# Filler matmuls on constants, a later bias transpose and a reordered tile norm in a two-model kernel on one core

## The chip, the cores and the metric

One core of one Trainium2 chip runs the whole program in one launch. The metric is the device time in microseconds, the median of the runs. The core has five engines with queues of their own: TensorE (PE; its weight loads are listed as PEld), VectorE (DVE), ScalarE (ACT), GpSimd (POOL) and SyncE (SP, which here only issues DMAs). They meet at semaphores. TensorE's clock has two levels, 1.2 and 2.4 GHz; the profile tells the granted one as a share of 2.4 (1.00 or 0.50, or between for a stretch that has both).

## The reference

Two models one after the other, all in float32. The first block has two layers over 256 latent tokens and, in layer 0, 256 context tokens, each 1024 wide. The second block has two layers over the 256 latent tokens.

```python
# first block, layer l
mod = silu(c) @ w_ada[l] + b_ada[l]                   # 6 x 1024 shifts, scales, gates; the same for c_ctx
h = modulate(rms_norm(x, norm1_g[l]), sh1, sc1)
y = mixer(h)       # w_in; Fourier mix, global and window attention; gated branches; w_out
x = x + g1 * y
h = modulate(rms_norm(x, norm2_g[l]), sh2, sc2)
aff = softmax(h @ w_router[l])                        # 16 experts
top_aff, top_idx = top_k(aff.T, 32)                   # each expert picks 32 of 256 tokens
out = (silu(xg @ w_gate_e) * (xg @ w_up_e)) @ w_down_e * top_aff
x = x + g2 * scatter_add(out)
# second block, layer l
h = rms_norm(x, attn_norm_g[l])
x = x + (three kinds of attention over h @ w_in, gated) @ w_out[l]
x = x + cross_attention(rms_norm(x, xattn_norm_g[l]), mem) @ w_xo[l]
```

Between the two blocks stands the first block's final norm with `final_g`, after the second a last one.

## The kernel before

Tokens lie in tiles of 128 partitions: tiles 0 and 1 are the latent set (set 0), 2 and 3 the context (set 1, layer 0 alone). All weights pass through a ring of four SBUF slabs of 2 MB. A list (`slab_plan`) sets their order; SP issues the load of slab i as soon as slab i - 4 was released, which TensorE does with `last_release` after its last matmul on it. The instruction order of every engine is written out by hand; a wait holds up all that stands behind it on its engine.

**Start (lines 2670 to 2681, 671 and 842).** ScalarE's queue loads the condition vectors and gains into `vec1`, then biases and norm gains into `vec0` and `PAIRED`. `turn_vectors` on TensorE turns `vec1` and then, after a wait for the second group of loads (`ld_vec0`), `PAIRED` twice and `vec0`. VectorE copies the first result, forms CT (the silu of the conditions), and then makes `vec0t` from the second with one copy and six small ones; all of that stands ahead of `mixer(0)`. There TensorE runs the products of the modulation: `ada_product(n)` multiplies CT with a slab of `w_ada`, 32 matmuls with 32 columns of weights each, listed as 64 instructions; a copy (`ada_row`), a transpose (`ada_turn`) and an addition of the bias (`ada_column`) follow. Products 0 and 2 come first, then the transposes of the normed tiles (`first_turn`), then `first_part`, the first projection.

**Ahead of the experts (lines 1051 to 1103).** In both layers TensorE turns tile 0, runs an ada product (18 or 22), `logits(0)`, `turn_tile(1)`, `ada_turn` and `logits(1)`: 8 matmuls of 16 columns against the router's weights, listed as 16 instructions. VectorE forms the softmax, and with a chain of small operations on 16 partitions (`eight` four times, `threshold`, `slots`) the list of tokens for each expert; `turn_slots` turns it, `first_selection` makes a 0/1 matrix of it, and `gather` multiplies with that. In layer 0 the context set goes first, so that `turn_slots(1)` and `gather(0, 1, h)` stand between the latent set's logits and its own `turn_slots(0)` and `gather(0, 0, h)`; ada products 19, 20 and 21 lie between. In layer 1 there is one set, product 23 and `scaled_rows`, which spreads the gate vector over the partitions. Then come the experts: per expert six slabs, four of gate and up weights (line 1146), two of down weights (line 1181).

**The second block (lines 1226 to 1484, 1847 to 1857, 2575 to 2590).** Each layer begins with the norm `n3` of both tiles: ScalarE squares and sums a tile and takes the root (`normed` in its program), VectorE scales it (`normed` in its own), TensorE turns it in eight transposes, and the two engines scale half of the turned blocks each into `HT2` (`gained`). The first group of the projection, G30, needs tile 0 alone. In layer 0 both tiles come from the first block's final norm. In layer 1 tile 1's X gets its last addition only from the last matmuls of the layer before (line 1366), tile 0's is complete before; both ScalarE and VectorE norm tile 1 before they scale tile 0's turned halves:

```python
            else:                                     # ScalarE, layer 1
                normed("n3@1", 0, XN2, [read("X00", 0), read("X10", 0)])
                normed("n3@1", 1, XN2, [at("xo_rd@0", 2)])
                gained("n3@1", 0, HT2, 24)
```

`unit` is the identity and `bars` holds attention masks, both in bf16 and constant from line 2087 on (but for two parts of `bars` that are not read by the change).

Of the kernel before, what the change touches and what calls it, by code (L numbers as in the profile page):

```python
# [23 lines left out]
P = 128  # L24
D = 1024
KC = D // P
SEQ = 256
DEPTH = 2
# [5 lines left out]
COL = 512  # L34
# [129 lines left out]
def build(nc, a, out, ctx):  # L164
# [11 lines left out]
    def at(name, value):  # L176

        return sem(name), value + signal(name)[1]
# [24 lines left out]
    vec0t = sb("vec0t", P)  # L203
# [467 lines left out]
    def _(pe):  # L671
        def turn_vectors():
            pe.wait_ge(*at("ld_vec1", 16 * VEC1_LOADS))
            pe.transpose(ps[1][:, 0:64], vec1[0:64, :], ident[0:64, 0:64]).then_inc(sem("vec_turned"), 1)
            pe.wait_ge(*at("ld_vec0", 16 * VEC0_LOADS))
# [38 lines left out]
        def last_release(pe):  # L714
            pe.drain().then_inc(slab_used, 1)  # L715

# [122 lines left out]
        def mixer(l):  # L839
            tokens = 4 * P if l == 0 else 2 * P  # L840
            if l == 0:
                ada_product(0)
                ada_turn(0)
                ada_product(2)
                for t in range(4):
                    for k in range(6):
                        first_turn(k, t)
# [100 lines left out]
        def experts(l):  # L948
# [130 lines left out]
            ada_turn(first, 2)  # L1079
            logits(1)  # L1080
            if l == 0:
# [9 lines left out]
            else:  # L1091
# [3 lines left out]
                scaled_rows()  # L1095
                turn_slots(0)
            gather(0, 0, 0)
# [123 lines left out]
        def block2(l):  # L1221
# [160 lines left out]

            pe.wait_ge(*at(f"n3@{l}_xn", 1))
            turn_tile(f"n3@{l}", 0, XN2)
            tile_ready(f"n3@{l}", 0)
# [100 lines left out]
        turn_vectors()  # L1486
# [10 lines left out]
    def _(act):  # L1497
# [275 lines left out]
        def block2(l):  # L1773
# [76 lines left out]
            else:  # L1850
                normed("n3@1", 0, XN2, [read("X00", 0), read("X10", 0)])
                normed("n3@1", 1, XN2, [at("xo_rd@0", 2)])
                gained("n3@1", 0, HT2, 24)
# [92 lines left out]
    def _(dve):  # L1946
# [82 lines left out]

        def rotate(v, cos, sin, h, w, temps):  # L2030
# [12 lines left out]
        def mixer(l):  # L2043
            tiles = range(4) if l == 0 else range(2)
            tokens = 4 * P if l == 0 else 2 * P
            if l == 0:
                n1_normed(0, 0)
                ada_row(0)
                n1_normed(0, 1)
# [372 lines left out]
        def block2(l):  # L2422
# [162 lines left out]
            normed(f"n3@{l}", 1, XN2)  # L2585
            for t in range(2):
                gained(f"n3@{l}", t, HT2, 16 + 8 * l)
# [85 lines left out]
        dve.wait_ge(*at("vec_turned", 2))  # L2673
        link(dve.tensor_copy(vec0t[:, :], ps[0][:, 0:P]))
        pairs_in = ps[0][:, P:P + 48].rearrange("p (i l n q) -> p l n q i", i=2, l=DEPTH, n=3)
        for l in range(DEPTH):
            for n, c in enumerate((24, 32, 56)):
                ins = dve.tensor_copy(vec0t[:, 64 * l + c:64 * l + c + 8].rearrange("p (q i) -> p q i", i=2),
                                      pairs_in[:, l, n])
        link(ins)  # L2680
# [67 lines left out]
```

## Time and profile before

| | us |
|---|---|
| three runs | 2294.29, 2292.11, 2294.47 |
| median | 2294.29 |
| the profiled execution | 2297.57 |
| its span, first to last instruction | 2295.7 |
| TensorE busy in the span | 1981.8 (86%) |
| VectorE, ScalarE busy | 623.4 (27%), 435.2 (19%) |
| mean granted clock | 0.961 |
| from HBM | 573 MB, 250 GB/s over the span |

A row of the timeline gives the start, the duration, the engine, the line, the operation, what it writes and reads, and in brackets how long the engine had been idle and what ended that. Neighbouring instructions of one line are merged (x16). A row of the stretches gives each engine's busy time, the granted clock (PEclk) and what the DMA moved. The duration of a pipelined matmul is longer than its distance to the next.

### The profile page before, as it was taken

What the parts mean: (1) busy time and instruction counts of PE and PEld (TensorE: products, weight loads), DVE (VectorE), ACT (ScalarE), POOL (GpSimd) and SP (SyncE); (2) the same over time, 40 slices, a digit from 0 to 9 for tenths busy, and PEclk for the clock granted to TensorE, in tenths of its full rate; (3) what the DMA queues carried; (4) which work ended last, traced back from release to release, by engine and by line L of the source; (5) the groups of instructions that cost most, each with busy time, mean ns of one, the idle gap of its engine ahead of it and who ended that gap; (6) DMA issues with size and microseconds to landing.
All of it is one profiled execution on the core that took longest, in us unless ns stands there. A gap on an engine that the chain in (4) does not pass through costs nothing.

```text
span 2295.7 us, 31442 instructions
## 1 busy us (share of the span) xinstructions
PE 1981.8 (86%) x13540; PEld 1088.4 (47%) x13540; DVE 623.4 (27%) x1483; ACT 435.2 (19%) x1095; POOL 26.9 (1%) x52
## 2 busy tenths in 40 slices
PE   6999999998988898889999975676776699989997
PEld 4445554455434444335768641233432247564765
DVE  2012640234112222213351321201110235323533
ACT  2112621013111111002261111100000212222222
POOL 3000000000000000000000000000000000000000
PEclk9999999999999999999999988889989899999999
DMA  8554245227899999994415589999999833233320
GB/s 288 183 175 157 73 147 183 74 73 277 344 423 422 422 422 421 416 418 149 147 46 187 217 348 423 424 415 416 417 414 418 333 110 110 103 118 110 110 83 19
DMA packets 133831, 576.01 MB, mean 251 GB/s; under 512 B 7448, under 2 KB 16128, under 8 KB 92736
## 3 DMA queue, kind: packets, MB, share of 16 engines
q1 hardware_dynamic: 129312, 556.82, 61.5%
q0 software_dynamic: 3872, 17.00, 2.2%
q8 instruction: 109, 1.79, 0.3%
q10 hardware_dynamic: 512, 0.19, 0.0%
q14 instruction: 26, 0.21, 0.0%
HBM read 572.93 MB, written 1.05 MB: 250 GB/s over the span
## 4 chain that ended last, share of the span: by engine, by line
PE 51%; DMA 20%; issue 10%; PEld 8%; DVE 5%; PEldq 3%; ACT 2%; SPq 0%; ACTq 0%; DVEq 0%
DMA ring<-w_up_e 15%; PE ps L781 8%; PE ps L1237 5%; PE ps L1146 5%; PE ps L964 4%; DMA ring<-w_down_e 3%; PE ps L1245 3%; PEld ps L1181 3%; PEldq L715 3%; PE ps L797 2%; PE ps L1379 2%; PE ps L770 2%; PEld ps L1015 1%; PE ps L1216 1%; PE ps L1322 1%
## 5 line engine op out<-in xcount | busy, mean ns | idle before, releaser
L1146 PE MATMUL ps<-ring,reg_bc 128*32 128x512 f32 x2960 | 381.8, 652 | 132.9 <-DMA ring<-w_up_e 124.8
L1146 PEld LDWEIGHTS ps<-ring,reg_bc 128*32 128x32 f32 x2960 | 91.6, 115 | 398.7 <-DMA ring<-w_up_e 208.1
L781 PE MATMUL ps<-reg_a,ring 128*128 128x512 f32 (+1 forms) x768 | 253.9, 488 | 6.1 <-issue 4.4
L781 PEld LDWEIGHTS ps<-reg_a,ring 128*128 128x128 f32 x768 | 143.5, 190 | 105.2 <-issue 92.2
L2323 DVE TENSOR_TENSOR xall<-xall,ps 128x512 f32<-128x512 f32 x48 | 32.8, 687 | 447.5 <-PE ps L1112 447.5
L1237 PE MATMUL ps<-ring,reg_a 128*128 128x512 f32 (+2 forms) x448 | 146.0, 482 | 7.4 <-issue 5.9
L1744 ACT ACTIVATE reg_bc<-ps 128x512 f32<-128x512 f32 x48 | 28.7, 597 | 571.2 <-PE ps L1146 571.2
L2366 DVE TENSOR_TENSOR reg_a<-ps,reg_e 32x256 f32<-32x256 f32 x192 | 80.7, 420 | 197.4 <-PE ps L1181 195.0
L1181 PE MATMUL ps<-ring,reg_bc 128*32 128x256 f32 x2048 | 117.4, 380 | 15.7 <-issue 13.3
L770 PE MATMUL ps<-ring,reg_a 128*128 128x512 f32 (+1 forms) x288 | 112.8, 546 | 1.9 <-issue 1.5
L1237 PEld LDWEIGHTS ps<-ring,reg_a 128*128 128x128 f32 x448 | 75.2, 193 | 72.2 <-issue 69.1
L1245 PE MATMUL ps<-reg_a,ring 128*128 128x256 f32 x384 | 90.7, 396 | 6.1 <-ACT reg_d L1782 5.0
L1181 PEld LDWEIGHTS ps<-ring,reg_bc 128*32 128x32 f32 x2048 | 69.7, 110 | 54.4 <-issue 19.4
L1181 PE MATMUL ps<-ring,reg_e 128*32 128x256 f32 x1024 | 63.4, 389 | 33.2 <-issue 17.6
L964 PE MATMUL ps<-ring,reg_bc 128*128 128x512 f32 x192 | 86.0, 604 | 0.6 <-issue 0.5
L797 PE MATMUL ps<-reg_d,ring 128*128 128x512 f32 (+1 forms) x256 | 84.2, 488 | 1.7 <-issue 0.8
L1245 PEld LDWEIGHTS ps<-reg_a,ring 128*128 128x128 f32 x384 | 75.2, 199 | 17.6 <-issue 7.0
L770 PEld LDWEIGHTS ps<-ring,reg_a 128*128 128x128 f32 x288 | 54.2, 190 | 56.2 <-issue 54.6
L797 PEld LDWEIGHTS ps<-reg_d,ring 128*128 128x128 f32 x256 | 48.1, 190 | 35.6 <-issue 30.4
L1552 ACT ACTIVATE reg_e<-ps 128x512 f32<-128x512 f32 (+1 forms) x48 | 23.6, 491 | 208.5 <-PE ps L781 208.4
L1181 PEld LDWEIGHTS ps<-ring,reg_e 128*32 128x32 f32 x1024 | 33.3, 111 | 56.4 <-issue 24.4
L566 DVE TENSOR_REDUCE st<-ps 128x2 f32<-128x1024 f32 (+1 forms) x36 | 37.5, 1046 | 82.7 <-PE ps L498 79.8
(354 smaller groups left out, 2145.7 us busy)
## 6 DMA issues: line engine op xcount, KB each, us to landing
ring<-w_down_e SPq DMA_DIRECT2D x64, 2048.0 KB, 15.2
ring<-w_gate_e SPq DMA_DIRECT2D x123, 1024.0 KB, 10.6
ring<-w_up_e SPq DMA_DIRECT2D x123, 1024.0 KB, 13.9
ring<-w_in SPq DMA_DIRECT2D x34, 2048.0 KB, 8.3
ring<-w_ada SPq DMA_DIRECT2D x24, 2048.0 KB, 8.1
ring<-w_out SPq DMA_DIRECT2D x8, 2048.0 KB, 8.1
ring<-w_xkv SPq DMA_DIRECT2D x8, 1024.0 KB, 14.1
ring<-w_br_global SPq DMA_DIRECT2D x4, 1024.0 KB, 6.2
```

Source lines behind the costliest of these rows:

```text
L566: ins = dve.tensor_reduce(neg, banks_of(2 * (i % 2), u["nk"]), X_AXIS, ALU.max, negate=True)
L715: pe.drain().then_inc(slab_used, 1)
L770: mm = pe.matmul(ps[t][:, c0:COL], HT[:, k, t * P:t * P + P], w[:, k, c0:COL], start=(k == 0), stop=(k == KC - 1))
L781: mm = pe.matmul(ps[j][:, 0:n], w[:, k, j * P:(j + 1) * P], HT[:, k, 0:n], start=(k == 0), stop=(k == KC - 1))
L797: mm = pe.matmul(ps[n % 4][:, 0:tokens], w[:, k, j * P:(j + 1) * P], OT[:, k, 0:tokens], start=(k == k0), stop=(k == k1 - 1))
L964: mm = pe.matmul(ps[b][:, :], MT[:, k, t * P:t * P + P], w[:, k, :], start=(k == 0), stop=(k == KC - 1))
L1146: mm = pe.matmul(ps[s][32 * j:32 * j + 32, :], XGT[l][:, e // 4, s, 2 * q + k, e % 4 * CAP:(e % 4 + 1) * CAP], w[j // 2][:, k, (j % 2) * C ...
L1181: mm = pe.matmul(ps[4 + s][32 * j:32 * j + 32, 0:SEQ], HE[l][:, s, k, q * CAP:(q + 1) * CAP], w[:, k, j * SEQ:(j + 1) * SEQ], start=(q == ...
L1237: fill(name, lambda b: [pe.matmul(ps[b][:, 0:c1 - c0], src[:, k, t * P:t * P + P], w[:, k, c0:c1], start=(k == 0), stop=(k == KC - 1)) for ...
L1245: fill(name, lambda b: [pe.matmul(ps[b][:, 0:SEQ], w[:, k, c * P:(c + 1) * P], src[:, k, :], start=(k == 0), stop=(k == KC - 1)) for k in ...
L1379: yield pe.matmul(ps[b][:, :], OT2[:, k, t * P:t * P + P], w[:, k, :], start=(q == 0), stop=(q == KC - 1))
L2366: ins = dve.tensor_tensor(OE[l][r:r + CAP, e // 4 % 2, s, j * SEQ:(j + 1) * SEQ], ps[4 + s][CAP * j:CAP * (j + 1), 0:SEQ], GB[CAP * j:CAP ...
```

## The change

It adds `keep_warm(b, n)` to TensorE's program: n matmuls with `unit` as stationary and 256 columns of `bars` as moving operand, into the second half of PSUM bank b, read by nobody. It is called at seven places: between `ada_turn` and `logits(1)` (24 in layer 0, 10 in layer 1), after `logits(1)` (10), in layer 1 after `scaled_rows` (8) and after `turn_slots(0)` (6), ahead of the second block's first wait in layer 0 (45), and after tile 0's transposes in both of its layers (14). `turn_vectors` is split: the condition vector is turned first as before, the biases only after `ada_product(0)`; their copies on VectorE move behind `ada_row(0)`, and TensorE waits for them after `ada_product(2)`. At the second block's second layer, ScalarE and VectorE scale tile 0's halves ahead of tile 1's norm.

```diff
-        def turn_vectors():
+        def turn_condition():
             pe.wait_ge(*at("ld_vec1", 16 * VEC1_LOADS))
             pe.transpose(ps[1][:, 0:64], vec1[0:64, :], ident[0:64, 0:64]).then_inc(sem("vec_turned"), 1)
+
+        def turn_biases():
             pe.wait_ge(*at("ld_vec0", 16 * VEC0_LOADS))
...
+        def keep_warm(b, n):
+
+            for _ in range(n):
+                pe.matmul(ps[b][:, SEQ:COL], unit[:, :], bars[:, 0:SEQ], start=True, stop=True)
...
                 ada_product(0)
+                turn_biases()
                 ada_turn(0)
                 ada_product(2)
+                pe.wait_ge(*at("vec0t", 1))
                 for t in range(4):
...
             ada_turn(first, 2)
+            keep_warm((4, 6)[l], (24, 10)[l])
             logits(1)
+            keep_warm((4, 6)[l], 10)
...
                 scaled_rows()
+                keep_warm(6, 8)
                 turn_slots(0)
+                keep_warm(6, 6)
             gather(0, 0, 0)
...
+            if l == 0:
+                keep_warm(7, 45)
             pe.wait_ge(*at(f"n3@{l}_xn", 1))
             turn_tile(f"n3@{l}", 0, XN2)
+            keep_warm(7, 14)
             tile_ready(f"n3@{l}", 0)
...
-        turn_vectors()
+        turn_condition()
...
                 normed("n3@1", 0, XN2, [read("X00", 0), read("X10", 0)])
+                gained("n3@1", 0, HT2, 24)
                 normed("n3@1", 1, XN2, [at("xo_rd@0", 2)])
-                gained("n3@1", 0, HT2, 24)
...
                 n1_normed(0, 0)
                 ada_row(0)
+                bias_columns()
                 n1_normed(0, 1)
...
-            normed(f"n3@{l}", 1, XN2)
-            for t in range(2):
-                gained(f"n3@{l}", t, HT2, 16 + 8 * l)
+                normed("n3@0", 1, XN2)
+                gained("n3@0", 0, HT2, 16)
+            else:
+                gained("n3@1", 0, HT2, 24)
+                normed("n3@1", 1, XN2)
+            gained(f"n3@{l}", 1, HT2, 16 + 8 * l)
```

`bias_columns` holds the seven copies that stood ahead of VectorE's layers, with the wait for the transposes before them and a signal (`vec0t`) behind.

## Rows read from the trace of the kernel before

**Rows 1.** The page: the chain that ended last, by engine, and GB/s in 40 slices.
```profile
PE 51%; DMA 20%; issue 10%; PEld 8%; DVE 5%; PEldq 3%; ACT 2%; SPq 0%; ACTq 0%; DVEq 0%
...
GB/s 288 183 175 157 73 147 183 74 73 277 344 423 422 422 422 421 416 418 149 147 46 187 217 348 423 424 415 416 417 414 418 333 110 110 103 118 110 110 83 19
```

**Rows 2.** Timeline of the start: SP's first issues, TensorE's transposes, products, first projection.
```profile
0.74 1.06 SPq L602 DMA_DIRECT2D ring<-w_ada  x2
...
16.20 0.43 PE L677 MATMUL ps<-ident,reg_e 24*128 24x24 f32 x2 [5.42 <-DMA reg_e<-norm_g]
...
16.97 3.64 PE L695 MATMUL ps<-ring,ct 128*32 128x128 f32 x64
...
21.43 2.45 PE L695 MATMUL ps<-ring,ct 128*32 128x128 f32 x64
...
24.03 2.83 PE L744 MATMUL ps<-ident,reg_d 128*128 128x128 f32 x24
...
28.58 7.10 PE L755 MATMUL ps<-ring,reg_a 128*128 128x512 f32 x16 [1.61 <-ACT reg_a L1513]
```

**Rows 3.** Ring loads, issue to landing: those under way in 0 to 1, 1 to 1.5 us.
```profile
DMA to landing us min/median/max: 13.0/13.0/13.0
...
DMA to landing us min/median/max: 13.0/16.0/18.9
```

**Rows 4.** Timeline of TensorE ahead of layer 0's experts.
```profile
529.86 1.93 PE L982 MATMUL ps<-wr,reg_a 128*128 128x16 f32 x16 [0.32 <-issue]
...
536.50 3.56 PE L982 MATMUL ps<-wr,reg_a 128*128 128x16 f32 x16 [3.53 <-issue]
...
549.90 2.04 PE L695 MATMUL ps<-ring,ct 128*32 128x128 f32 x64 [0.31 <-ACT modt L1535]
...
552.13 0.29 PE L997 MATMUL ps<-ident,reg_e 16*128 16x16 f32 x2 [0.18 <-DVE reg_e L2233]
...
553.24 4.04 PE L1015 MATMUL ps<-tmp,reg_d 128*128 128x128 f32 x32 [0.55 <-DVE tmp L2240]
```

**Rows 5.** Stretches: busy time of PE, PEld, DVE, ACT, POOL; PEclk, DMA share, GB/s.
```profile
1308.00:1312.00 4.00, 2.71 (x18) 2.26 (x17) 2.10 (x5) 2.12 (x8) 0.00 (x0) 0.67 1.01 424
...
1332.00:1336.00 4.00, 4.00 (x31) 2.56 (x30) 0.00 (x0) 2.77 (x8) 0.00 (x0) 0.85 0.00 0
...
1338.00:1800.00 462.00, 311.38 (x2408) 138.88 (x2408) 57.62 (x146) 37.92 (x84) 0.00 (x0) 0.88 1.01 418
...
2061.00:2064.00 3.00, 3.00 (x6) 1.21 (x5) 0.00 (x0) 0.00 (x0) 0.00 (x0) 0.55 0.23 85
```

**Rows 6.** Timeline of TensorE ahead of layer 1's experts.
```profile
1311.96 3.57 PE L982 MATMUL ps<-wr,reg_a 128*128 128x16 f32 x16 [1.29 <-ACT reg_a L1669]
...
1327.68 0.27 PE L997 MATMUL ps<-ident,reg_e 16*128 16x16 f32 x2 [1.11 <-DVE reg_e L2233]
...
1328.77 5.57 PE L1015 MATMUL ps<-tmp,reg_d 128*128 128x128 f32 x32 [0.81 <-DVE tmp L2240]
```

**Rows 7.** Timeline at the second block's first layer: last X addition, tile 0's transposes, G30.
```profile
1815.62 0.69 DVE L2323 TENSOR_TENSOR xall<-xall,ps 128x512 f32<-128x512 f32 x1 [0.17 <-PE ps L1112]
...
1821.98 1.94 PE L1256 MATMUL ps<-ident,reg_d 128*128 128x128 f32 x8 [6.41 <-DVE reg_d L2446]
...
1825.19 8.58 PE L1237 MATMUL ps<-ring,reg_a 128*128 128x512 f32 x16 [1.27 <-ACT reg_a L1787]
```

**Rows 8.** Timeline at the second block's second layer: transposes, VectorE's half, G30.
```profile
2054.75 1.09 PE L1256 MATMUL ps<-ident,reg_d 128*128 128x128 f32 x8
...
2058.39 1.12 DVE L2440 TENSOR_SCALAR reg_a<-ps,vec1t 128x128 f32<-128x128 f32 x4
2059.62 8.80 PE L1237 MATMUL ps<-ring,reg_a 128*128 128x512 f32 x16 [3.77 <-issue]
```

**Rows 9.** The bf16 mask matmuls: durations (min/median/max ns) by line, four in the timeline.
```profile
L1279 PE MATMUL ps<-bars,unit x80: 219/219/230, 1864.8 to 2200.1; 128*128 128x128 bf16 x80
...
1864.81 0.40 PE L1279 MATMUL ps<-bars,unit 128*128 128x128 bf16 x4
```

## What the change should do to the time: a prediction

> **What bounds the kernel now.** First the page: its chain of waits gives TensorE half of the span and the DMA a fifth [rows 1], and the row of GB/s shows two plateaus near 420, the two expert stages, with weaker slices before and after. From 1338 to 1800 us the DMA moves 418 GB/s without a pause [rows 5]: there a faster TensorE buys nothing. What comes before such a plateau still counts, if the stream is waiting for TensorE: from 1332 to 1336 it moved 0 GB/s [rows 5], since no ring slab had been released. The same holds for layer 0, where slices 9 and 10 (516 to 631 us) stand at 277 and 344 GB/s [rows 1]. So I read the timeline at the five places that the diff touches, and beside it the granted clock in the table by stretches. At each, TensorE waits, its clock falls from 2.4 to 1.2 GHz, and the work behind the wait pays for it: 16 matmuls of the logits take 1.93 us at full clock and 3.56 at half [rows 4], 16 of the projection 7.10 [rows 2] against 8.58 and 8.80 [rows 7, 8].
>
> **What a filler costs.** None is in the trace. Its nearest relative is the bf16 mask matmul of 128 columns on the same stationary `unit`: one alone lasts 0.22 us and four in a row 0.40, so each further one costs (0.40 - 0.22) / 3 = 0.06 us [rows 9]. A filler has 256 columns: 0.11 us at full clock, 0.23 at half. 10 cost 1.1, 14 cost 1.6, 24 cost 2.7, 45 cost 5.1 us. They read constants and write halves of banks that nobody reads then, so nothing but TensorE's own queue is behind them.
>
> **Start.** Before, three bias transposes stand ahead of the first ada product and wait 5.4 us for the last small load, until 16.20; the product starts at 16.97 [rows 2]. Its slab was there at 0.74 + 13.0 = 13.7 us [rows 2, 3]. Now it runs 13.8 to 17.4, the biases follow without a wait, and the second product starts when its slab lands, 18.9 us after an issue at about 1.2 us [rows 3]: 20.1 instead of 21.43. VectorE's seven short bias copies move behind `ada_row(0)`; TensorE's new wait `vec0t` has all the first transposes queued behind it, but stands behind the second product, which can't start before 20.1 and so covers the copies; without that cover they would hold the transposes up by their own length. In exchange TensorE, which had nearly unbroken work from 16.97, now has 2.7 us between the products with only four small transposes in it. The second product took 2.45 before [rows 2]; a product costs 3.64 at half clock and 2.04 at full [rows 2, 4]. At 3.64 it ends at 23.8, as before (23.9); at 2.04, 1.7 us earlier; and if the clock is still low behind it, the 24 transposes cost up to 2.8 us more [rows 2]. Ends: +1.7 and -2.8. I take -0.2, by the row of the cold product, since a pause comes in where the clock had been rising. On SP's queue the first released slab's load is issued earlier, but behind three loads that are still under way (18.9 us to landing [rows 3]), so it lands no earlier.
>
> **Layer 0 before the experts.** The 24 fillers (2.7 us) stand in an idle stretch of 3.53 us ahead of the second logits [rows 4]. They hold the clock: 3.56 becomes 1.93, +1.6. The next ten (1.1 us) delay `turn_slots(1)`, for which VectorE's first selection waits, with token set 0's top-k queued behind it: -0.3. The third ada product gets faster, but VectorE's chain to the second `slots` is what TensorE waits for; so what is late next is that chain, and TensorE, about 1.5 us ahead of it, now idles there after its product of 549.90 [rows 4]. Before, it had no gap there (552.13 with 0.18 us of waiting). No filler covers this new gap, and behind it stand gathers of 4.04 us [rows 4]; in layer 1 the same work took 5.57 with the clock partly low [rows 6]. Ends: +1.6 and, with gathers wholly at half clock, about -2.5. I take +1.3 - 1.5 = -0.2.
>
> **Layer 1 before the experts.** The clock is already falling before the first ten fillers (0.67 from 1308 to 1312 [rows 5]), so they cost up to 2.3 us in a gap of 1.29 [rows 6]: the logits start 1.0 late and then take 1.93 instead of 3.57: +0.6. The second ten lie beside the softmax; the 8 beside VectorE's chain, where TensorE idles 1.11 us; the 6 (0.7 us) in the 0.81 us before the gather [rows 6]. The gathers should take 4.04 [rows 4] instead of 5.57 [rows 6]: +1.5. I take +2.0; ends 0 (clock lost twice) and 3.1 (never lost). It passes to the end, since the stream starts with the first slab released.
>
> **First seam of the second block.** The last X addition ends at 1816.3; TensorE transposes again at 1821.98 [rows 7]. 45 fillers end at 1821.4, so they fit; if that cover went, their excess would be paid in full. The 8 transposes fall from 1.94 to about 1.09 [rows 7, 8], of which I count 0.4, since VectorE's norm of tile 1 still stands ahead of its half of the copies. The 14 more (1.6 us) lie beside the copies. G30's 8.58 becomes 7.10: +1.5. Sum +1.9; ends +0.4 and +2.4.
>
> **Second seam.** Here the order changes too. Tile 0 is transposed from 2054.75 to 2055.84; VectorE scales its half only at 2058.39, for 1.12 us, behind tile 1's norm, and G30 starts at 2059.62 [rows 8]. Now both halves follow the transposes: 2055.9 + 1.12 = 2057.0; the 14 fillers end at 2057.3. G30 starts 2.3 earlier and takes 7.10 instead of 8.80 (clock 0.55 in 2061 to 2064 [rows 5]): +1.7. Tile 1's norm starts about 1 us later on both engines, since each now scales tile 0 first, but TensorE asks for it only after G30, 7 us on. Together +4.0; ends +2.0 (the order alone, with 0.3 lost) and +4.2.
>
> **Sum.** -0.2 - 0.2 + 2.0 + 1.9 + 4.0 = 7.5 us. The profiled execution took 2297.57, so it would be 2290.1; the median of the runs before is 2294.29, 3.3 less, and I carry that difference over: **2286.8 us**. Its own range, with one or two places falling well or badly: 2284 to 2289.7. This kernel's measurement can tell about 0.2% (4.6 us) from no change.
>
> **Rivals.**
> Everything holds: the upper ends, but in layer 0 the 1.3 without the gap's cost: 1.7 + 1.3 + 3.1 + 2.4 + 4.2 = 12.7 gives 2281.6. Against it: the new gap in layer 0. Chance 0.11.
> Transposes don't count as work for the clock. The trace shows 8 transposes in 1.09 us where 8 others took 1.94 [rows 7, 8], so they follow the clock, not whether they hold it. If they do nothing for it, the second seam is bridged by 14 fillers alone and the start has 24 transposes with nothing to lift the clock: 1.7 and, as the middle of what cold transposes cost, 1.3 less: total 4.5, 2289.8. Chance 0.10. The Trainium skill, page "TensorE: Matmul & The Clock Gate", section "Part 4: PE-mode transpose", states that the full clock does not engage for transposes, which don't count as busy in the same way; by that rule this case is the one, while the trace at least contradicts that they run slow.
> The start and layer 0 fall badly (-2.8, -2.5) and layer 1 gives 0: with 1.9 and 4.0 at the seams 0.6 us, 2293.7. For it: in both places work was moved or shortened and an idle stretch of 2 to 3 us left behind it that no filler covers. Chance 0.11.
> The fillers don't hold the clock and only the new order pays: 2.3 - 0.3 = 2.0, 2292.3. Against it: unbroken small matmuls did raise the clock at the start, where one product took 3.64 and the next 2.45 [rows 2]. Chance 0.07.
> The other side, slower: the fillers run at 1.2 GHz, 0.23 us each. Then the 45 take 10.3 us in 5.6, 4.7 late, and the 14 behind them (3.2) 1.9 more than the copies beside them; in layer 0 24 take 5.5 in 3.5 and ten 2.3 against 1.2 that are hidden, 3.1; in layer 1 1.0 + 0.9 + 0.6 = 2.5; start 0.2; less 0.7 at the second seam: 11.7 slower, 2306.0. It decides at the first seam: above 5.6 / 45 = 0.125 us for one filler the change begins to lose. Against it: the bf16 row at full clock [rows 9], and TensorE works until 0.7 us before the 45. Chance 0.05.
>
> **Chances.** Forecast 0.56, the others as given. Range 2281.5 to 2292.5: it leaves out the bad case and the slower one, 0.16. Faster than 2289.7: 0.56 (less 0.01), 0.11 and half of the transpose case: 0.72. Slower 0.05, within 0.23.
>
> **What would show it.** Right: 45 fillers in about 5 us ending before 1821; G30 7.1 us at both seams, starting near 2057 less what was gained before; logits 1.93; layer 1's first slab released 2 us earlier against its start. Wrong: fillers over 0.125 us each; gathers at 553 above 5 us (then layer 0 has cost something, as I suspect) or at 4.04 (then I was too low); the 24 first transposes above 3 us.

## The result, and the profile after

The changed kernel took **2283.57 us** (median, 2280.98 to 2284.23) against 2294.38 for the kernel before on the same chip: ratio 0.995, 95% interval 0.9933 to 0.9967, so 10.8 us or 0.5% faster. A second comparison (the run `changed_again` below) gave 2281.87 against 2293.82, ratio 0.9955 (0.9942 to 0.9969). The prediction said 2286.8 with a range of 2281.5 to 2292.5, and faster with a chance of 0.72.

The profiled execution after took 2280.98 us (span 2279.1), the one before 2297.57. These two differ by 16.6 us, more than the medians; where the rest lies is a question of its own, taken up below. First the places that the diff touches. (`keep_warm` is called by six statements, not seven as said above; with both layers they run nine times.) All rows are of the timeline of TensorE: start and duration in us, line, operation, number of instructions, and in brackets the idle time ahead and what ended it.

The start, after:

```profile
13.50 3.64 PE L697 MATMUL ps<-ring,ct 128*32 128x128 f32 x64 [2.92 <-DMA ring<-w_ada]
...
20.12 3.64 PE L697 MATMUL ps<-ring,ct 128*32 128x128 f32 x64 [0.94 <-DMA ring<-w_ada]
24.06 3.68 PE L751 MATMUL ps<-ident,reg_d 128*128 128x128 f32 x24 [0.29 <-DVE reg_d L1992]
...
29.45 4.10 PE L762 MATMUL ps<-ring,reg_a 128*128 128x512 f32 x9 [1.60 <-ACT reg_a L1529]
```

The first product now starts at 13.50, as soon as its slab has landed, and the second at 20.12, 1.3 us earlier than before [rows 2]. But both take 3.64 us, and the transposes behind them 3.68. That this is the half clock can't be read from the profile's column of the granted clock, which gives 1.00 for all of the start. Two other things show it. The same product took 3.64 us in the kernel before at 1317.50, where that column gives 0.50:

```profile
1317.50 3.64 PE L695 MATMUL ps<-ring,ct 128*32 128x128 f32 x64
```

```profile
1317.60:1321.00 3.40, 3.40 (x64) 2.86 (x64) 3.22 (x10) 0.12 (x1) 0.00 (x0) 0.50 0.95 390
```

And the trace's list of clock changes begins with a rise to full: at 22.5 us before, inside the second product, and at 25.9 after, inside the transposes. The projection starts at 29.45.

Layer 0 ahead of the experts, after:

```profile
529.82 2.78 PE L722 MATMUL ps<-bars,unit 128*128 128x256 bf16 x24
533.49 1.93 PE L991 MATMUL ps<-wr,reg_a 128*128 128x16 f32 x16 [0.89 <-issue]
...
547.39 0.29 PE L1006 MATMUL ps<-ident,reg_e 16*128 16x16 f32 x2 [1.54 <-DVE reg_e L2262]
548.50 5.37 PE L1024 MATMUL ps<-tmp,reg_d 128*128 128x128 f32 x32 [0.55 <-DVE tmp L2269]
```

The 24 fillers take 2.78 us, 0.11 each, and the logits behind them 1.93 instead of 3.56 [rows 4]. The slots (L1006) now wait 1.54 us, which they did not before, and the gathers behind that wait take 5.37 instead of 4.04 [rows 4].

Layer 1 ahead of the experts, after, and two lines of the table by stretches (columns: stretch, length, busy time of PE, PEld, DVE, ACT and POOL with their instructions, granted TensorE clock, DMA share, GB/s):

```profile
1303.96 2.18 PE L722 MATMUL ps<-bars,unit 128*128 128x256 bf16 x10
1305.98 1.86 PE L991 MATMUL ps<-wr,reg_a 128*128 128x16 f32 x16
...
1319.68 0.39 PE L1006 MATMUL ps<-ident,reg_e 16*128 16x16 f32 x2 [2.81 <-DVE reg_e L2262]
1320.01 1.46 PE L722 MATMUL ps<-bars,unit 128*128 128x256 bf16 x6
1321.26 4.67 PE L1024 MATMUL ps<-tmp,reg_d 128*128 128x128 f32 x32
```

```profile
1303.00:1307.00 4.00, 4.00 (x26) 3.40 (x25) 1.37 (x4) 2.12 (x8) 0.00 (x0) 0.64 1.02 422
1807.00:1813.00 6.00, 5.09 (x45) 4.32 (x45) 5.62 (x17) 4.87 (x13) 0.00 (x0) 1.00 1.05 387
```

The clock is already down when the first ten fillers start, as it was before them before (0.64 in 1303 to 1307, against 0.67 [rows 5]); they take 2.18 us, almost twice their price, but the logits take 1.86 instead of 3.57 and the gathers 4.67 instead of 5.57 [rows 6]. The wait ahead of the slots (L1006) is not gone: it is 2.81 us, behind the eight fillers, where it was 1.11 [rows 6].

The first seam of the second block, after:

```profile
1807.53 5.09 PE L722 MATMUL ps<-bars,unit 128*128 128x256 bf16 x45 [0.78 <-DVE xall L2352]
1813.06 1.09 PE L1269 MATMUL ps<-ident,reg_d 128*128 128x128 f32 x8 [0.45 <-DVE reg_d L2475]
1813.99 1.69 PE L722 MATMUL ps<-bars,unit 128*128 128x256 bf16 x14
1815.90 7.11 PE L1250 MATMUL ps<-ring,reg_a 128*128 128x512 f32 x16 [0.21 <-issue]
```

45 fillers in 5.09 us, 0.45 us before the norm is ready; transposes 1.09 instead of 1.94, G30 7.11 instead of 8.58 [rows 7].

The second seam, TensorE and then VectorE:

```profile
2042.53 1.09 PE L1269 MATMUL ps<-ident,reg_d 128*128 128x128 f32 x8
2043.45 1.69 PE L722 MATMUL ps<-bars,unit 128*128 128x256 bf16 x14
2044.98 7.03 PE L1250 MATMUL ps<-ring,reg_a 128*128 128x512 f32 x16
```

```profile
2043.65 1.13 DVE L2469 TENSOR_SCALAR reg_a<-ps,vec1t 128x128 f32<-128x128 f32 x4 [0.50 <-PE ps L1269]
...
2046.50 0.81 DVE L2475 TENSOR_SCALAR reg_d<-xall,st 128x1024 f32<-128x1024 f32 x1
```

VectorE scales tile 0's half (L2469) right behind the transposes, and tile 1's norm (L2475) follows; G30 starts 2.45 us after the start of the transposes instead of 4.87 and takes 7.03 instead of 8.80 [rows 8].

**What one pair of traces can't say.** Of the 16.6 us, the places of the diff give 7.3 by the lengths below (-0.9, 0.4, 1.7, 1.8, 4.2). The other 9.3 lie where nothing was edited. The clearest such place is H4 and H5, 32 matmuls of the second block's projection, run in each of its layers, behind the same wait of 2.48 us in both traces, before and after:

```profile
1968.75 10.20 PE L1245 MATMUL ps<-reg_a,ring 128*128 128x256 f32 x32 [2.48 <-ACT reg_d L1782]
```

```profile
1957.99 8.73 PE L1258 MATMUL ps<-reg_a,ring 128*128 128x256 f32 x32 [2.48 <-ACT reg_d L1798]
```

Behind one and the same wait the clock may fall for a while (8.73) or for longer (10.20); traces further down show it stay as well (7.14). So each place has to be read in several executions, and the experiments gave these.

### The profile page after: what moved, and what is told of

Its sections match the earlier page's. It is cut to its first block, busy times and chain, and to the rows that moved or that the text cites. A ratio compares the mean times of both kernels' runs of the same rounds, so it can differ in the third digit from the quotient of the medians.

```text
span 2279.1 us, 31723 instructions
## 1 busy us (share of the span) xinstructions
PE 1986.8 (87%) x13681; PEld 1093.5 (48%) x13681; DVE 623.2 (27%) x1483; ACT 435.3 (19%) x1095; POOL 26.9 (1%) x52
## 4 chain that ended last, share of the span: by engine, by line
PE 53%; DMA 19%; issue 10%; PEld 8%; DVE 5%; PEldq 2%; ACT 2%; SPq 0%; POOL 0%; DVEq 0%; POOLq 0%
DMA ring<-w_up_e 14%; PE ps L788 8%; PE ps L1159 6%; PE ps L1250 5%; PE ps L973 4%; PE ps L1258 3%; PEld ps L1194 3%; PE ps L804 2%; PE ps L1392 2%; PE ps L777 2%; PEldq L717 2%; DMA ring<-w_xkv 2%; DMA ring<-w_down_e 2%; PE ps L1226 1%; PE ps L1229 1%
## 5 line engine op out<-in xcount | busy, mean ns | idle before, releaser
L1194 PE MATMUL ps<-ring,reg_bc 128*32 128x256 f32 x2048 | 117.8, 380 | 16.2 <-issue 14.7
L1194 PE MATMUL ps<-ring,reg_e 128*32 128x256 f32 x1024 | 67.2, 406 | 31.4 <-issue 17.6
L1194 PEld LDWEIGHTS ps<-ring,reg_e 128*32 128x32 f32 x1024 | 34.5, 116 | 57.1 <-issue 29.2
L1705 ACT ACTIVATE reg_bc<-ps,modt,scl 128x128 f32<-128x128 f32 x96 | 36.2, 458 | 129.2 <-PE ps L1024 129.2
```

Source lines behind the costliest of these rows:

```text
L1194: mm = pe.matmul(ps[4 + s][32 * j:32 * j + 32, 0:SEQ], HE[l][:, s, k, q * CAP:(q + 1) * CAP], w[:, k, j * SEQ:(j + 1) * SEQ], start=(q == ...
L1705: ins = act.activation(XGT[l][:, g, s, k, :], ps[6 + h][:, kk * P:(kk + 1) * P], ACT.Identity, scale=SCL[:, l, 1, k, s:s + 1], bias=MODT[: ...
```

## The experiments

**A place's length over all executions.** The lengths used below are: *start*, the time at which the first projection starts; *layer 0*, from the first tile's logits of the place to the first expert matmul; *layer 1*, from the transposes ahead of its logits to the first expert matmul; *first and second seam*, from tile 0's transposes to tile 1's. Each is read from the profiled execution of each kernel. The numbers in brackets are means. The kernels below that add fillers in a place or warm the start are left out of that place's row. The one whose fillers are transposes is in the rows of the start and the first seam only.

```
                 without the edit                     with the edit
start            28.58 28.14 28.0 27.2 27.76  (27.9)  29.45 27.0 28.47 28.60 29.65 28.41 28.37  (28.6)
layer 0          29.67 30.04 29.68 30.75 29.92 (30.0) 29.28 27.98 27.98 30.01 29.03 29.49       (29.0)
layer 1          30.77 31.44 31.49 31.41      (31.3)  29.04 28.98 29.11 29.66 29.23 and 4 like them (29.2)
first seam       11.62 11.95 12.20 11.88      (11.9)  9.76 to 9.78, nine executions
second seam      13.50 14.75 14.81           (14.35)  order alone 9.30, fillers alone 11.80, both 9.32
```

**The kernel before, once more.** No edit; a second trace of it.

> The kernel before, unedited, for a second trace of it. The first two traces (before 2297.57, after 2280.98) differ by 16.6 us where the medians differ by 10.8 to 12. Theory 1 (the rest is which of the unchanged pauses the clock fell behind in those two executions): this execution lies nearer to the median of 2294, and H4 and H5 at 1969, which took 10.20 us, come out at 7.1 or 8.8; the stretches that the diff touches keep their lengths within 1.5 us (layer 1's place 30.8, first seam 11.6, second seam 13.5). Theory 2 (the stretches differ by the kernel's own order, not by execution): the same 10.20 at H4 and H5, and the same stretch lengths within 0.3 us everywhere.

Measured: median 2294.87 (2292.07 to 2299.56) against 2294.73 for its twin, ratio 0.9999 (0.999 to 1.0008); the profiled execution took 2299.56. So "nearer to the median" was a miss, this was another long one. The lengths of the places were not the same within 0.3 us, which rules the second theory out (layer 1's place is 31.44 instead of 30.77, the second seam 14.75 instead of 13.50): H4 and H5 took 8.70 instead of 10.20, G30 at the second seam 10.06 instead of 8.80 [rows 8].

```profile
1970.94 8.70 PE L1245 MATMUL ps<-reg_a,ring 128*128 128x256 f32 x32 [2.48 <-ACT reg_d L1782]
...
2060.29 10.06 PE L1237 MATMUL ps<-ring,reg_a 128*128 128x512 f32 x16 [3.77 <-issue]
```

**The changed kernel, once more.** No edit.

> The changed kernel itself, unedited, as the measure for the other two kernels on the same chip. Ratio to the kernel before as in the first comparison, 0.995, within its interval of 0.9933 to 0.9967. If it stands at 0.997 or above, a part of the first 10.8 us was luck of which pauses the clock fell behind.

Measured: the ratio 0.9955 given above, as expected. Its trace bears on the suspicion about layer 0's new wait:

```profile
548.04 0.30 PE L1006 MATMUL ps<-ident,reg_e 16*128 16x16 f32 x2 [1.53 <-DVE reg_e L2262]
...
549.15 4.04 PE L1024 MATMUL ps<-tmp,reg_d 128*128 128x128 f32 x32 [0.55 <-DVE tmp L2269]
```

The same wait of 1.53 us, and the gathers take 4.04. Of the five traces in which that wait is there (1.25 to 1.54 us) and nothing fills it, three have 4.04 and two 5.37 and 5.57. The wait costs about 1.5 us in some executions and nothing in others. In two more traces the clock had fallen earlier, from the second logits on (2.3 us instead of 1.93); there the wait is gone (0.17 us), since TensorE comes later, and the gathers take 4.04. Of these seven traces only two, this one and that of the doubled fillers further down, held the clock through the whole place. They have its shortest length, 27.98; in the other five the clock fell somewhere, at the transposes, the logits, the fillers or the gathers, and the place took 29.0 to 30.0.

In layer 1 the same trace has all of it at full clock up to the slots, and the fall behind them:

```profile
1318.01 0.39 PE L1006 MATMUL ps<-ident,reg_e 16*128 16x16 f32 x2 [2.81 <-DVE reg_e L2262]
1318.34 1.46 PE L722 MATMUL ps<-bars,unit 128*128 128x256 bf16 x6
1319.59 5.67 PE L1024 MATMUL ps<-tmp,reg_d 128*128 128x128 f32 x32
```

Of the ten traces with layer 1's fillers, six have the first ten at half clock (2.2 to 2.3 us) and four at full (1.25). The gathers took 4.04 in one of the ten, 4.7 to 6.0 in the others, and longest (5.7 to 6.0) in the four whose first ten fillers had run at full clock. So the place is 29.0 to 29.7 us long either way.

**The start alone.** `turn_condition`, `turn_biases` and `bias_columns` as in the change; no fillers, the old order at the seam:

```diff
-        turn_vectors()
+        turn_condition()
...
                 ada_product(0)
+                turn_biases()
                 ada_turn(0)
                 ada_product(2)
+                pe.wait_ge(*at("vec0t", 1))
```

> The kernel before with the start's edit alone (biases turned behind the first ada product), no fillers, old order at the second seam. My account: no gain, between 0.9 us slower (as the first projection in the profile of the changed kernel, 29.45 against 28.58 us) and 0.5 faster; the second ada product begins near 20.1 us and takes 3.6, the 24 first transposes take more than the 2.83 us of before. Rival (the earlier products pay): the first projection begins at 27.2 or earlier and the whole is 1.4 to 1.7 us faster.

Measured: 2293.68 (2291.92 to 2297.12) against 2296.27, ratio 0.9992 (0.9984 to 1.0001): no change that can be told; the interval runs from 0.2 us slower to 3.7 us faster. In this execution the clock rose at 18.1, the second product took 1.96 and the projection started at 27.0, the best of all; in six others with this edit that product took 2.89 to 3.64 and the projection started at 28.4 to 29.7. In all five traces without the edit the second product took 1.95 to 2.45.

**The order alone.** Only ScalarE's and VectorE's order at the second seam:

```diff
                 normed("n3@1", 0, XN2, [read("X00", 0), read("X10", 0)])
+                gained("n3@1", 0, HT2, 24)
                 normed("n3@1", 1, XN2, [at("xo_rd@0", 2)])
-                gained("n3@1", 0, HT2, 24)
```

> The kernel before with the second seam's new order alone, no fillers. G30 begins 1.5 us after the transposes instead of 3.8. My account: 2.3 us from the order; whether the clock holds over the shorter idle stretch decides on another 1.6: 2.3 to 4.0 us faster than before. Rival (the fillers carry that seam): the clock falls there in this kernel too, G30 takes 8.6 us or more, and the whole is 2.3 us faster at most.

Measured: 2290.08 (2286.67 to 2293.24), ratio 0.9972 (0.9963 to 0.9982), 6.2 us by the medians, more than the 2.3 to 4.0 expected. The seam takes 9.30 us, 5.0 less than the mean of 14.35, with no filler in the kernel:

```profile
2048.13 1.09 PE L1261 MATMUL ps<-ident,reg_d 128*128 128x128 f32 x8
2050.48 7.11 PE L1242 MATMUL ps<-ring,reg_a 128*128 128x512 f32 x16 [1.26 <-ACT reg_a L1792]
```

A wait of 1.26 us is left, and G30 behind it runs at full clock. That is one trace, but the medians of eight runs agree: the interval begins at 4.1 us, above the 2.5 that the order gives without the clock.

**The fillers alone.** All calls of `keep_warm`, without the start's edit and with the old order.

```diff
+            keep_warm((4, 6)[l], (24, 10)[l])
             logits(1)
+            keep_warm((4, 6)[l], 10)
...
+                keep_warm(7, 45)
...
             turn_tile(f"n3@{l}", 0, XN2)
+            keep_warm(7, 14)
```

> The kernel before with all fillers, without the start's edit and the new order. My account by places: layer 0 +0.4 (gathers at 548 to 553 us partly at half clock), layer 1 +1.7, first seam +1.9, second seam +1.6 by the clock alone: 5.6 us faster. Rival (the changed kernel's 10.8 us come from fillers acting beyond their places): 8 us or more.

Measured: 2287.24 (2286.65 to 2288.18), ratio 0.9962 (0.9949 to 0.9975), 9.0 us (5.7 to 11.7), where 5.6 was expected and 8 or more by the rival. By the means in the table the places of this kernel give 1.0 + 2.2 + 2.1 + 2.6 = 7.9 us, so most of the difference is that the 5.6 was added up from one pair of traces; fillers that act beyond their places aren't needed for it. The second seam takes 11.80:

```profile
2046.09 1.09 PE L1265 MATMUL ps<-ident,reg_d 128*128 128x128 f32 x8
2047.02 1.69 PE L720 MATMUL ps<-bars,unit 128*128 128x256 bf16 x14
2050.95 7.11 PE L1246 MATMUL ps<-ring,reg_a 128*128 128x512 f32 x16 [2.24 <-issue]
```

Here the fillers end and a wait of 2.24 us for VectorE is left, which is what the new order takes away (11.80 - 9.32 = 2.5 us); G30 is at full clock in either kernel. So at this seam each half is enough for the clock, in the one trace that each has, and once the order is new, the 14 fillers show no gain of their own (9.30 without them, 9.32 with them).

**The change without the start's edit.**

```diff
-        turn_condition()
+        turn_vectors()
```

(with the rest of the start as before.)

> The changed kernel without the start's edit. If the start costs, as its profile says (0.9 us at the first projection), this is 0.9 us faster than the changed kernel, 11 to 12 us faster than before. If the start pays, it is 1 to 2 us slower than the changed kernel, 9 to 10 us faster than before.

Measured: 2284.32 (2279.28 to 2287.46), ratio 0.9946 (0.9933 to 0.996). The whole change had 0.995 and 0.9955: with or without the start's edit, no difference can be told.

**The change without layer 0's 34 fillers.**

```diff
-            keep_warm((4, 6)[l], (24, 10)[l])
+            if l:
+                keep_warm(6, 10)
             logits(1)
-            keep_warm((4, 6)[l], 10)
+            if l:
+                keep_warm(6, 10)
```

> The changed kernel without the 24 and the 10 fillers of layer 0; all others stay. It measures the term that the prediction took as -0.2 us (ends +1.6 and -2.5). Theory 1 (the prediction's): the second logits 3.56 instead of 1.93, no wait ahead of the second slots, gathers 4.04: within 0.5 us of the changed kernel. Theory 2 (the fillers of layer 0 gain, since what is late next is hidden better than I thought): 1 to 1.6 us slower. Theory 3 (they cost): up to 2.5 us faster than the changed kernel. In the profile: from the first logits of the place to the first expert matmul 29.3 us in the changed kernel (22.64 and 6.64) and 29.7 before.

Measured: 2285.39 (2282.95 to 2287.95) against 2281.87 for the changed kernel in the same runs, 3.5 us slower; the two intervals of their ratios overlap (0.9952 to 0.9977, and 0.9942 to 0.9969), so the size is not sure, but the sign agrees with the place: 29.92 us here, 30.0 in the mean of the five without these fillers, 29.0 in the mean of the six with them. The two groups overlap (29.67 to 30.75, and 27.98 to 30.01).

```profile
534.43 3.57 PE L991 MATMUL ps<-wr,reg_a 128*128 128x16 f32 x16 [3.53 <-issue]
...
550.27 0.29 PE L1006 MATMUL ps<-ident,reg_e 16*128 16x16 f32 x2
...
551.36 4.04 PE L1024 MATMUL ps<-tmp,reg_d 128*128 128x128 f32 x32 [0.50 <-DVE tmp L2271]
```

The rows of before are back: logits 3.57 behind an idle stretch of 3.53, and no wait at the slots, as both theories have it. The size is nearer to the second, with about 1 us by the place.

**Do transposes hold the clock?** Every filler becomes a transpose of the identity, their numbers unchanged:

```diff
-                pe.matmul(ps[b][:, SEQ:COL], unit[:, :], bars[:, 0:SEQ], start=True, stop=True)
+                pe.transpose(ps[b][:, SEQ:SEQ + P], ident[:, :], ident[:, :])
```

> The changed kernel with every filler made a transpose of the identity (float32, 128 columns) instead of a bf16 matmul, the numbers of them unchanged. Eight real transposes took 1.09 us in the changed kernel, so 45 should take 5.0 to 5.5 us, as the fillers' 5.09. Theory 1 (transposes keep the clock up as well as matmuls do; for it, the run with the order alone, where nothing but transposes stood between O and G30 and G30 still took 7.1): logits 1.93 in both layers, G30 7.1 at both seams, 2284 us, within 0.1% of the changed kernel. Theory 2 (transposes do not count, as the Trainium skill, page "TensorE: Matmul & The Clock Gate", section "Part 4: PE-mode transpose", states): the second logits of layer 0 back to 3.56, layer 1's logits to 3.57 and its gathers to 5.6, the first G30 to 8.6: 1.6 + 3.1 + 1.5 = 6 us slower, 2289.8.

Measured: 2285.25 (2283.91 to 2287.76), ratio 0.9963 (0.9951 to 0.9976).

```profile
1811.64 5.13 PE L722 MATMUL ps<-ident 128*128 128x128 f32 x45 [0.78 <-DVE xall L2352]
...
1820.01 7.10 PE L1250 MATMUL ps<-ring,reg_a 128*128 128x512 f32 x16 [0.20 <-issue]
```

45 transposes last 5.13 us, and G30 behind them 7.10. The places: layer 0 29.5, layer 1 29.2, seams 9.76 and 9.32, each as with matmuls. The first theory holds: float32 transposes keep the clock as well as bf16 matmuls do. The ratio is 0.0008 to 0.0013 above the changed kernel's, inside the intervals.

**Twice the fillers at the first seam.**

```diff
-                keep_warm(7, 45)
+                keep_warm(7, 90)
```

> The changed kernel with 90 fillers instead of 45 at the first seam. In the changed kernel 45 take 5.09 us from 1807.5 and the norm's first tile is ready at 1813.06. Theory 1 (a filler past its cover is paid in full, and the clock is full at either count): the 90 end at 1817.7, the transposes start 4.6 us later, G30 still takes 7.1: 2288.2. Theory 2 (what ends last at the seam is VectorE's or the DMA's chain, so an excess is partly hidden): under 2 us slower, 2284 to 2285.5. Theory 3 (fillers at half clock): 0.23 us each, the 90 take 20 us, 15 us slower.

Measured: 2288.83 (2285.26 to 2294.98), ratio 0.9975 (0.9964 to 0.9986), 0.20 to 0.25% above the changed kernel's ratios, which is 4.6 to 5.7 us; the intervals still touch.

```profile
1808.01 10.00 PE L722 MATMUL ps<-bars,unit 128*128 128x256 bf16 x90 [0.78 <-DVE xall L2352]
1817.85 1.04 PE L1269 MATMUL ps<-ident,reg_d 128*128 128x128 f32 x8
...
1820.25 7.03 PE L1250 MATMUL ps<-ring,reg_a 128*128 128x512 f32 x16
```

10.00 us for 90, the same 0.11 each. From the first expert matmul of layer 1 to the transposes it takes 491.4 us instead of 487.0 to 487.7 (488.7 in one of nine), and the seam behind 9.27 instead of 9.77: 3.7 us net, paid almost in full, as the first theory has it. The cover of 5.6 us is real and has 0.45 left.

**Three more waits filled.**

```diff
                 ada_product(20, 2)
+                keep_warm(6, 12)
                 turn_slots(0)
...
+            keep_warm(4, 20)
             columns("H4", "in2", 7, 2, HT2)
```

> The changed kernel with fillers in three more waits that the clock falls behind: 12 ahead of layer 0's second slots (they wait 1.54 us, and the gathers behind took 5.37 instead of 4.04), and in both layers 20 ahead of H4 in the second block (wait 2.48 us; H4 and H5 behind it took 8.73 and 8.59, where 32 such matmuls take 7.2 at full clock). Theory 1 (the fall follows from the pause right ahead, and filling it takes the fall away): gathers 4.04, H4 and H5 7.2, 1.3 + 1.5 + 1.4 = 4.2 us, 2279.4. Theory 2 (the falls are only moved on to the next pause): the same total as the changed kernel within 1 us. Theory 3 (the fillers run over their pause): 0 to 1 us slower.

Measured: 2284.04 (2282.85 to 2285.84), ratio 0.9956 (0.9945 to 0.9968): no better than the changed kernel. The two kinds of wait part:

```profile
537.80 2.26 PE L722 MATMUL ps<-bars,unit 128*128 128x256 bf16 x10
...
549.86 1.48 PE L722 MATMUL ps<-bars,unit 128*128 128x256 bf16 x12
...
552.38 4.04 PE L1024 MATMUL ps<-tmp,reg_d 128*128 128x128 f32 x32 [0.56 <-DVE tmp L2271]
```

```profile
1960.64 2.35 PE L722 MATMUL ps<-bars,unit 128*128 128x256 bf16 x20
1963.28 7.14 PE L1259 MATMUL ps<-reg_a,ring 128*128 128x256 f32 x32 [0.29 <-ACT reg_d L1800]
```

In layer 0 the gathers take 4.04, but the clock has fallen earlier, at the ten fillers behind the logits (2.26 us instead of 1.25), and the place is 29.3 us long, as without the twelve. That is what the second theory forecast, but it doesn't show it: this earlier fall stands ahead of the twelve, and traces without them have it too, so what they do to the clock stays open. Ahead of H4 the first theory holds. Without fillers, 22 executions of this stretch (eleven traces, two layers) gave 7.14 three times, 8.5 to 8.8 seventeen times and 10.20 twice, in the mean 8.65; with them, 7.14 in six of six. That is 1.5 us in each layer by the place. The median does not show these 3 us.

**The same, with the start warmed.** Float32 matmuls of the identity on itself ahead of the first product (12), and 3 and 4 around the transpose of its row:

```diff
+                warm_up(12)
                 ada_product(0)
                 turn_biases()
+                warm_up(3)
                 ada_turn(0)
+                warm_up(4)
                 ada_product(2)
```

> The kernel with the three filled pauses, and in addition float32 matmuls of the identity on itself at the start: 12 ahead of the first ada product, 3 before and 4 after the transpose of its row. Theory 1 (the clock rises before the first product): the products 2.04 us instead of 3.64, the second from 20.1 to 22.2, the first transposes limited by VectorE's last norm at 23.8, the first projection at 27.3 instead of 29.45: 2.2 us, 2277.2. Theory 2 (the gain at the start is taken back, since the projection's slabs or the vector engines' chain set what follows): projection starts earlier, but the first logits near 505 do not; 2279.4. Theory 3 (not enough work to lift the clock): products 3.6 each, no gain.

Measured: 2280.29 (2278.34 to 2284.02), ratio 0.9943 (0.993 to 0.9956), 3.75 us below the kernel without the warm start in the same runs, with intervals that overlap. The clock rose at 14.7 us. The products took 1.96 us each, the projection started at 27.09 and the first logits at 503.7; in the seven traces with the start's edit alone these logits start at 504.6 to 506.6. The 12 ran 4.85 us and held the first product up until 15.40, which cost nothing, since the second waits for its slab until 20.3.

**The warm start with 7, 1 and 3 matmuls, H4's fillers, nothing added in layer 0.**

```diff
-                warm_up(12)
+                warm_up(7)
...
-                keep_warm(6, 12)
                 turn_slots(0)
```

> The changed kernel with 20 fillers ahead of H4 in both layers, and float32 matmuls of the identity at the start (7 ahead of the first product, 1 and 3 around the transpose of its row; 0.40 us each where the clock was half, so 7 take 2.8 of the 2.9 us that TensorE waits for the slab). Nothing is added in layer 0 ahead of the slots. Theory 1 (both gains add, and the start's 2.3 us pass on to the end): H4 and H5 7.2 instead of 8.7 twice, 3.0, projection at 27.1 instead of 29.45, 2.3: 5.3 us below the changed kernel in the same runs. Theory 2 (the start's gain is taken back before the first logits): 3.0 us below it. Theory 3 (the falls of the clock move elsewhere): within 1 us of it.

Measured: 2282.47 (2278.13 to 2286.48), ratio 0.9952 (0.9938 to 0.9965), against 2281.87 for the changed kernel in the same runs.

```profile
10.62 3.35 PE L678 MATMUL ps<-ident 128*128 128x128 f32 x14
13.90 2.89 PE L701 MATMUL ps<-ring,ct 128*32 128x128 f32 x64
...
20.28 1.95 PE L701 MATMUL ps<-ring,ct 128*32 128x128 f32 x64 [0.58 <-DMA ring<-w_ada]
22.53 2.81 PE L755 MATMUL ps<-ident,reg_d 128*128 128x128 f32 x24 [0.29 <-DVE reg_d L2000]
...
27.06 6.26 PE L766 MATMUL ps<-ring,reg_a 128*128 128x512 f32 x14 [1.60 <-DMA ring<-w_in]
```

Its profiled execution, 2278.13 us, is the shortest seen, with projection at 27.06, logits at 503.6 and H4 at 7.14 twice, just what was expected place by place. The median of its five runs gives none of it: by the medians the third theory. Five runs of each, spread over 4 to 8 us, can't tell 5 us from nothing here, and `gaps_start` points the other way. Whether the two additions pay stays open, and so does how much of the start's gain reaches the first logits: these two traces have them at 503.6 and 503.7, but one without the start's edit and without any warming has them at 503.8, though its projection starts at 27.76.

## Why the prediction was right

**The price of a filler**: right. 0.11 us at full clock, in tens, 24s, 45 and 90; 0.22 at half. (The working as shown, 0.06 us for 128 columns, would give 0.12 for 256; the 0.11 is what was measured.)

**Start**, -0.2 with ends +1.7 and -2.8: the size was a little too kind, -0.7 by the mean of the projection's starts (27.9 to 28.6), with the spread that the ends gave (27.0 to 29.65). The step was right: the second product starts when its slab lands, and loses in the clock what it gains in time. That the clock is the cause is shown by the executions in which it rose early and stayed, at 18.1 in the start alone and at 14.7 and 15.9 with the warm start: there the same order reaches the projection at 27.0 and 27.1. In three more traces with this edit it rose at 16.4 to 17.6, but fell again at 19.8 to 21.0, about the pause between the products, and the second product took 2.9 to 3.5. What the step costs the whole kernel stays open: the start alone, with an interval of -0.2 to +3.7 us, doesn't show the loss of 0.7.

**Layer 0**, -0.2: the term that was most mis-sized; it is +1.0. The logits went from 3.56 to 1.93 and the new wait of 1.5 us appeared, both as worked out. The step that was off is the 1.5 taken for slow gathers: they come in two of seven traces. In three others the clock falls elsewhere in the place, and only two are free of a fall.

**Layer 1**, +2.0: 31.3 to 29.2, 2.1. The number is right, the way to it only in part, and that is luck. The sum had +1.5 for gathers at 4.04, and they took 4.04 in one of ten traces. The wait of 1.11 us ahead of the slots, which the eight fillers were to cover, was a row of one execution: in the other three traces without fillers it is 3.0, and with them 2.8 are left in nine of ten, the fall of the clock behind it. Without fillers the gathers took 5.57, 6.68, 6.59 and 6.74, so there was more to gain than the sum knew; and the logits gave more than the 0.6 where the first ten fillers ran at full clock, in four of ten. These errors cancel.

**First seam**, +1.9: 11.9 to 9.8, 2.1. The fillers fit into 5.6 us; G30 7.1. Doubling them showed both the cover and the price beyond it, on which the case "slower" rested.

**Second seam**, +4.0 (2.3 order, 1.7 clock): 14.35 to 9.32, 5.0. The order is worth 2.5. The clock's term was read from one execution with G30 at 8.80; two other traces have 10.06 and 10.12, in the mean 9.66 instead of 7.1, 2.6 us. What the prediction had not seen is that the new order alone holds the clock (G30 7.11 behind 1.26 us of waiting), so the parts are not added: the order alone 5.0, the fillers alone 2.6, both 5.0. So the +1.7 has the right cause, a clock that is held, but the new order is enough to hold it.

**Sum**: -0.7 + 1.0 + 2.1 + 2.1 + 5.0 = 9.5 us by the places, 7.5 predicted, 10.8 and 11.9 by the medians. Their intervals (7.6 to 15.4 and 7.1 to 13.3 us) hold the 9.5; the 7.5 lies at their lower edge. The other 9.3 us of the first pair of traces lay in stretches that nobody edited: 3.3 between the logits at 505 and those at 530 (24.7 us before, 21.4 after; all traces of either order have 21.4, 23.1 or 24.7), 1.5 at H4, and 3.3 between layer 0's first expert matmul and layer 1's logits, the rest in pieces of 0.2 to 0.5. Whether a small part of the medians' gain comes from such stretches too isn't settled.

**The rival that transposes don't count**: out. It would have brought G30 back to 8.6 in the kernel whose fillers are transposes; it took 7.10, and in the kernel with the order alone 7.11. The Trainium skill, page "TensorE: Matmul & The Clock Gate", section "Part 4: PE-mode transpose", says that the full clock does not engage for transposes; the measurement decides against that here, for float32 transposes of 128 columns, 45 of which kept the clock for 5.13 us (granted clock 1.00 from 1811.7 to 1816.7). **That the fillers don't hold the clock**: out, by the fillers alone (ratio 0.9962). **Start and layer 0 fall badly**: the start's edit alone is at 0.9992, and layer 0 gains. **Everything holds** (2281.6): nearer to the medians than the forecast, but not for its reason, since the start didn't gain and the clock fell in layer 1. (The chance of faster adds up to 0.71, not 0.72.)

## What to carry to other kernels

Where TensorE waits for a known chain of another engine and dense work follows, work on constants in that wait can keep the clock for 0.11 us a piece, if it ends before the chain does: past that point nearly all of it is paid. It did so in every trace at the two seams and at H4. Ahead of the experts, where narrow matmuls and several short waits follow one another, it held the clock throughout in two of seven traces in layer 0 and in none of ten in layer 1. Before filling a wait, see whether a change of order takes it away, since that gave both the wait and the clock back. And read such a gain place by place in several traces: behind one and the same wait the clock fell in most executions, not in all, and a length taken from one trace was off by 0.9 us at the second seam (13.50, mean 14.35) and by 1.5 us the other way at H4 (10.20, mean 8.65).

## What the runs showed of the hardware that was not expected

A wait of 2.48 us ahead of the same 32 matmuls cost 0, 1.5 or 3.1 us (7.14, about 8.7, 10.20), in 3, 17 and 2 of 22 executions; 20 fillers in it made it 0 in six of six. After the 24 fillers of layer 0 the clock still fell in five of the nine traces that have them, at or behind the logits (16 instructions of 16 columns, after a wait of 0.9 us), so the ten fillers that follow took 2.2 to 2.4 us instead of 1.25. In a sixth it had fallen before them, and the 24 took 3.63. The clock also falls without a pause: beside or right behind the first 32 such instructions of logits, at 505 us, with 0.3 us of idle time ahead, it fell in nine of fourteen traces (0.72 in 505 to 510 before, 1.00 after), which makes the 21.4 us to the next logits 23.1 or 24.7. That the narrow matmuls are the reason was not tested. And one and the same kernel spreads over 9 us and more between its executions (2290.66 to 2299.5 in 17 of the kernel before, 2285.26 to 2294.98 in 12 with the doubled fillers), as much as most single edits here are worth.
